# The input projection of a decoder step by a Strassen scheme: seven half-width products in place of eight

## The chip, the cores and the metric

The kernel runs on one core of one Trainium2 chip. The metric is the device time of one execution in microseconds (us). TensorE multiplies, VectorE and ScalarE read its banks in PSUM and work on SBUF, GpSimd clears buffers and issues gathers, and the queue of SP issues most DMA transfers. All numbers of the computation are f32.

## What is computed

One layer for a prompt of 256 tokens and 64 sample tokens (8 requests of 8 tokens), with 2048 features. The part that matters here is the first projection, and what is taken from it:

```python
h = rmsnorm(x, lw['g_attn_norm'])
z = h @ w_in            # 2048 x 4656; columns: q 1024, kc vc ks vs kw vw 256 each, gates 48, u 1024, v 1024
q_rot = partial_rope(q, q_pos)          # also for ks and kw
u = gelu(u)
v = rmsnorm(gelu(v), lw['g_sgu_v'])
```

After it come the compression of cached keys and values, selected and windowed attention, a gated mixing of tokens, an output projection, attention to a memory of 256 tokens (its keys and values are projected ahead of `h @ w_in`) and a mixture of 16 experts.

## The kernel before

The kernel is a row of blocks of code, one for each stage, with a barrier of all engines between them. In the first stage the inputs are normalised and transposed into `hT` (128 lanes x 16 chunks x 320 tokens: feature chunks on the lanes), and the memory's keys and values are made in `mem_kv`. The second stage is the input projection. Its start is at 80.5 us of the profile and the barrier behind it ends at 424 us.

The 4656 columns are worked on in ten blocks, in the order Q0, KS, Q1, KW, KC_, V2, V1, UV, GU, U1. The first five are 512 columns wide, V2 is 416 and the others are 420. A block's weights are 16 chunks of 128 features by its columns. They lie in one of two buffers: `wbuf[0]` is `raw`, which the next stage fills with gathered cache pages, and `wbuf[1]` is `w_in1`. `load(n)` on SP (L426) fetches block n once block n-2 has been multiplied, so it is a block ahead.

For each block `multiply(n)` on TensorE makes three outputs: the prompt's token tiles 0 and 1 (128 tokens each, 16 matmuls of the whole width, L490), and tile 2 with the 64 sample tokens, whose two halves of the columns go to the two halves of the lanes (32 matmuls, L494). Tile r is in bank `4 * (n % 2) + r`. ScalarE takes them from there (L562, with the gelu for u and v), and VectorE takes tile 1 of the blocks KS, KW and KC_ (L610), makes `QR` from `QQ` and applies the rope to q, ks and kw (L592 to L595).

After the blocks KS, KW and KC_ TensorE also turns finished rows into columns, in `turn_blocks(n)` (L506). Each job is up to four transposes into bank 3 or bank 7, by turns, and a copy out of it by `copy_jobs` (L396): even jobs by ScalarE, odd ones by VectorE. A job waits until the job two before it is copied:

```python
if k >= 2:
    pe.wait_ge(copied[k % 2], k // 2)
```

Jobs 0 and 1 are the memory's keys (`m_jobs`, within KS), 2 to 7 are q of Q0 (within KS), 8 to 13 are q of Q1 (within KW), 14 to 16 are the keys (KC_). On VectorE `take(n)` and then `copy_jobs(n)` follow each other for each block. After UV the position rows of the compression are transposed (`pe_terms`, L513), after GU they are multiplied (`pe_sums`, L520), and at the end turned into a column (`pe_columns`, L526). SP stores finished keys and values between its loads, and after the load of V1 it loads the weights of the compression. ScalarE's queue issues two copies of cached windows from DRAM to DRAM (4 MB each) once the first tile is made. GpSimd clears the unused lanes of `QQ` and `Z` at the start (L468, L469) and issues the first two gathers of cache pages into `raw` (L205) when the last block that uses `raw` is multiplied. `vjunk` takes the squares of v, which nothing reads.

Of the kernel before, what the change touches and what calls it, by code (L numbers as in the profile page):

```python
# [21 lines left out]
P = 128  # L22
KC = D // P
# [25 lines left out]
IN_COLS = 4656  # L49
NMEM = 256  # L50
# [99 lines left out]
def trunk(nc, A, out, scratch, const_at):  # L150
    top = ExitStack()
    with top:
# [30 lines left out]
        ident = cst("ident")  # L183
        gain_attn = sb(top, "gain_attn", [P, KC])
# [15 lines left out]
        raw = raw_scope.enter_context(nc.sbuf_tensor("raw", [P, 2, STRIDE * KVW], F32, side="right"))  # L200
        raw_loaded = [sem(f"raw_loaded{u}", True) for u in range(2)]

        def gather_cmp(pool, turn):
# [8 lines left out]
        pe_rows, peT, pe_bias = right("pe_rows", [KC, 2, P]), right("peT", [P, 2, KC]), right("pe_bias", [P, 2])  # L212
# [5 lines left out]
                in_scope.enter_context(nc.sbuf_tensor("w_in1", [P, KC, 512], F32, side="right"))]  # L218
        w_in = w_view("w_in")
        w_in_loaded = sem("w_in_loaded")  # L220

        with ExitStack() as scope:
# [4 lines left out]
            ms = sb(scope, "start_ms", [P, 5])  # L227
# [15 lines left out]
            with nc.Block() as block:  # L243
                @block.sync
                def _(sp):
# [11 lines left out]
                    sp.dma_start(const[:, P:], A["const"][:, P:]).then_inc(const_loaded, 16)  # L257
# [6 lines left out]
                    sp.dma_start(wbuf[0][:, :, :], w_in[:, :, 0:512]).then_inc(w_in_loaded, 16)  # L264
# [92 lines left out]
        with ExitStack() as scope:  # L357
            QQ, QR = (w1[:, :, :, :].rearrange("p u c n -> p (u c n)")[:, a:a + TILES * 512].rearrange("p (r n) -> p r n", n=512) for a in (0, TILES * 512))
            vgain = sb(scope, "vgain", [P, SW])
            ta = sb(scope, "rope_a", [P, 128])  # L360
            tb = sb(scope, "rope_b", [P, 128])
            vjunk = sb(scope, "vjunk", [P, SW])
            vms = sb(scope, "vms", [P, TILES])
            loaded = [w_in_loaded, sem("w_in_loaded1")]
            ready = [sem(f"w_in_ready{u}") for u in range(2)]
            taken_a, taken_d, roped, turned, v_squared, v_scaled, v_rooted, v_ready, gated, vgain_loaded, state_out, blank_q = (sem("w_in_" + x) for x in (
                "taken_a", "taken_d", "roped", "turned", "v_squared", "v_scaled", "v_rooted", "v_ready", "gated", "vgain_loaded", "state_out", "blank_q"))
# [7 lines left out]
            for n, k in ((V2, 4), (V1, 3), (UV, 2), (U1, 1), (GU, 0)):  # L375
                COLS[n] = (Q_COLS + GUV[k], GUV[k + 1] - GUV[k])
# [12 lines left out]
            JOBS = {KS: m_jobs + q_jobs(0), KW: q_jobs(1), KC_: k_jobs}  # L389
            J_BEFORE = {n: sum(len(JOBS.get(m, ())) for m in range(n)) for n in range(NT_IN + 1)}  # L390
# [7 lines left out]
            with nc.Block() as block:  # L398
                @block.sync
                def _(sp):  # L400
# [21 lines left out]
                    def load(n):  # L422
                        a, width = COLS[n]
                        if n >= 2:
                            sp.wait_ge(ready[n % 2], TILES * (n // 2))
                        sp.dma_start(wbuf[n % 2][:, :, 0:width], w_in[:, :, a:a + width]).then_inc(loaded[n % 2], 16)  # L426

                    load(1)
                    sp.dma_start(vgain[:, :], A["g_sgu_v"][0].partition_broadcast(P)).then_inc(vgain_loaded, 16)
                    for n, kind in enumerate(("mem_k_p", "mem_v_p")):  # L430
                        for r in range(2):
                            store(out[kind][0, 0, r * P:(r + 1) * P].rearrange("r h d -> r (h d)"),
                                  mem_kv[:, r, n * MW:(n + 1) * MW])
                    for n in range(2, NT_IN):
                        load(n)
                        done = n - 2
                        if done in (KS, KW, KC_):
                            sp.wait_ge(taken_a, done + 1)
                            sp.wait_ge(taken_d, done + 1)
                            if done != KC_:  # L440
                                sp.wait_ge(roped, done + 1)
# [11 lines left out]
                        if n == V1:  # L453
# [21 lines left out]
                def _(pe):  # L475
                    def multiply(n):
# [3 lines left out]
                        if n >= 2:  # L480
                            pe.wait_ge(taken_a, n - 1)
                            if n - 2 <= KC_:
                                pe.wait_ge(taken_d, n - 1)
# [2031 lines left out]
```

## Time and profile before

| | us |
|---|---|
| median of 3 runs | 1654.53 (1652.16 to 1656.22) |
| the profiled execution | 1652.59 |
| its span, first to last instruction | 1650.8 |
| the input projection with its barrier (80.58 to 424.04) | 343.46 |
| TensorE busy in it | 336.11 |
| VectorE busy in it | 22.79 |
| ScalarE busy in it | 32.50 |

An f32 matmul has two records in the profile, one for each of its passes, and a transpose has one. The records overlap, so the pace of a series is read from the starts of its groups, not from the mean duration. "PEld" is the load of the stationary operand, and "x" counts records. The mean granted clock of TensorE over the whole span is 0.924 of 2.4 GHz.

### The profile page before, as it was taken

The numbers are of one execution on the slowest core, as the hardware profiler recorded it, in microseconds if no ns is written. First come the engines' busy times: TensorE is split into PE (matmuls) and PEld (weight loads), VectorE is DVE, ScalarE is ACT, GpSimd is POOL, SyncE is SP. The second block draws the span as 40 slices with busy tenths as digits, with TensorE's granted clock in tenths as the row PEclk, the third lists the DMA queues.
The fourth block names the chain that finished last, engine by engine and source line by source line (L and its number), as shares of the span: only waits on it lengthen the run. The fifth ranks groups of instructions, "written<-read, shape, count | busy, mean of one in ns | idle before, by whom it ended". The sixth has DMA issues, their size and how long they took to land. (4 is left out here: it accounts for less than half of the span.)

```text
span 1650.8 us, 19858 instructions
## 1 busy us (share of the span) xinstructions
PE 1443.3 (87%) x7384; PEld 794.2 (48%) x7385; DVE 387.3 (23%) x972; ACT 296.7 (18%) x667; POOL 83.5 (5%) x111
## 2 busy tenths in 40 slices
PE   7999999999999988878899999859879978699890
PEld 4444445556788756644444575533323333233330
DVE  3101010000365265466310212521100100101015
ACT  3000000011333234357100113201000000000001
POOL 0000000000200000000000000001001010010100
PEclk9999999999999689979899999969989988899895
DMA  9276224252242077500943222979998999979975
GB/s 357 104 303 254 103 99 139 99 173 103 103 153 65 22 220 229 158 12 1 340 135 110 94 102 103 388 276 401 392 415 307 414 404 388 416 309 414 414 299 195
DMA packets 112657, 371.89 MB, mean 225 GB/s; under 512 B 17331, under 2 KB 55259, under 8 KB 82919
## 3 DMA queue, kind: packets, MB, share of 16 engines
q1 hardware_dynamic: 106898, 334.88, 53.5%
q0 software_dynamic: 5552, 27.89, 4.9%
q10 hardware_dynamic: 144, 8.26, 1.2%
q8 instruction: 42, 0.69, 0.2%
q14 instruction: 21, 0.17, 0.0%
HBM read 394.60 MB, written 26.49 MB: 255 GB/s over the span
## 5 line engine op out<-in xcount | busy, mean ns | idle before, releaser
L2359 PE MATMUL bank<-ring,hT_e 128*64 x576 | 251.7, 595 | 8.2 <-DMA ring<-in_w_exp_up 6.8
L2360 PE MATMUL bank<-ring,hT_e 128*64 128x512 f32 x576 | 251.9, 595 | 0.0
L2376 PE MATMUL bank<-W,const 128*64 128x512 f32 x576 | 150.2, 677 | 53.1 <-DMA W<-in_w_exp_down 48.6
L2359 PEld LDWEIGHTS bank<-ring,hT_e 128*64 128x64 f32 x576 | 78.5, 138 | 167.7 <-issue 167.7
L490 PE MATMUL bank<-raw,hT 128*128 128x512 f32 (+1 forms) x320 | 131.6, 573 | 0.6 <-PEq L243 0.6
L490 PE MATMUL bank<-w_in,hT 128*128 128x512 f32 (+2 forms) x320 | 123.7, 547 | 0.0
L2376 PEld LDWEIGHTS bank<-W,const 128*64 128x64 f32 x576 | 45.0, 155 | 145.0 <-issue 100.5
L1715 PE MATMUL bank<-W,mixT 128*128 128x512 f32 x256 | 113.4, 603 | 1.6 <-DVE mixT L1950 1.6
L490 PEld LDWEIGHTS bank<-raw,hT 128*128 128x128 f32 x320 | 61.5, 193 | 67.5 <-issue 67.3
L490 PEld LDWEIGHTS bank<-w_in,hT 128*128 128x128 f32 x320 | 60.4, 190 | 61.0 <-issue 61.0
L1715 PEld LDWEIGHTS bank<-W,mixT 128*128 128x128 f32 x256 | 49.0, 193 | 63.5 <-issue 61.4
L2360 PEld LDWEIGHTS bank<-ring,hT_e 128*64 128x64 f32 x576 | 78.5, 138 | 0.0
L2422 DVE SCALAR_TENSOR_TENSOR gate<-bank,row_w,gate 64x512 f32<-64x512 f32 x18 | 13.6, 757 | 257.8 <-ACT gate L2402 257.8
L2428 DVE COPY const<-bank 128x512 f32<-128x512 f32 x18 | 12.4, 692 | 198.9 <-PE bank L2376 198.9
L2402 ACT ACTIVATE gate<-bank 64x512 f32<-64x512 f32 x18 | 10.6, 589 | 244.2 <-PE bank L2360 244.2
L2336 POOL DMA_INDIRECT scratch_moe_y<-const,to_row x36 | 35.9, 998 | 365.8 <-DVE const L2428 360.3
L732 PE MATMUL bank<-const,rawg 128*128 128x128 f32 (+1 forms) x320 | 48.0, 273 | 3.2 <-ACT rawg L792 3.2
L2348 PE MATMUL bank<-const,x 64*128 64x64 f32 x304 | 37.9, 277 | 13.2 <-DMA x<-scratch_hn,from_row 13.2
L2348 PEld LDWEIGHTS bank<-const,x 64*128 64x128 f32 x304 | 35.3, 202 | 28.2 <-issue 28.2
L2407 ACT COPY const<-bank 128x512 f32<-128x512 f32 x18 | 10.6, 586 | 198.2 <-PE bank L2376 198.2
L732 PEld LDWEIGHTS bank<-const,rawg 128*128 128x128 f32 (+1 forms) x320 | 39.4, 152 | 12.5 <-ACT rawg L792 3.3
L999 PE MATMUL bank<-const,k_in 128*128 128x128 f32 x192 | 30.1, 306 | 14.3 <-DVE keyT L1079 4.8
(403 smaller groups left out, 1782.5 us busy)
## 6 DMA issues: line engine op xcount, KB each, us to landing
ring<-in_w_exp_gate SPq DMA_DIRECT2D x80, 1024.0 KB
ring<-in_w_exp_up SPq DMA_DIRECT2D x72, 1024.0 KB
W<-in_w_exp_down SPq DMA_DIRECT2D x72, 1024.0 KB
raw<-in_w_in SPq DMA_DIRECT2D x3, 4096.0 KB
W<-in_w_out SPq DMA_DIRECT2D x3, 4096.0 KB, 13.3
w_in<-in_w_in SPq DMA_DIRECT2D x2, 4096.0 KB, 14.7
k_in<-in_cache_sel_k SPq DMA_DIRECT2D x64, 128.0 KB
v_in<-in_cache_sel_v SPq DMA_DIRECT2D x64, 128.0 KB, 3.5
```

The lines of the kernel that those rows point to most:

```text
L490: mm = pe.matmul(bank[4 * u + r][:, 0:width], hT[:, c, r * P:(r + 1) * P], w, start=(c == 0), stop=(c == KC - 1))
L732: mm = pe.transpose(bank[k % LEAD][:, g * n:g * n + n], rawg[0:n, q // 4, a:a + P], ident[0:n, 0:n])
L999: mm = pe.transpose(bank[4 + n % 2][:, k * P:k * P + P], k_in[:, 4 * m + k, c * P:c * P + P], ident)
L1715: mm = pe.matmul(to, hT[:, c, r * P:r * P + P], w(c, slice(0, 512)), start=(c == 0), stop=(c == chunks - 1))
L2336: pool.indirect_dma_start(out=y_rows, out_offset=bass.IndirectOffsetOnAxis(ap=to_row[:, u, h:h + 1], axis=0), in_=y[:, u, h, :], in_offset ...
L2348: mm = pe.transpose(bank[6 + h][:, k * NS:k * NS + NS], rows_in[:, 8 * h + k:D:KC], ident[UP, UP])
L2359: pe.matmul(bank[4 + u][0:NS, :], hT[:, u, c, :], w_g[:, c, :], start=(c == 0), stop=(c == KC - 1))
L2360: mm = pe.matmul(bank[4 + u][UP, :], hT[:, u, c, :], w_u[:, c, :], start=(c == 0), stop=(c == KC - 1))
L2376: mm = pe.matmul(bank[2 * u + n // 2][lane, :], actT[:, q, :], w_d[:, q, 512 * n:512 * n + 512], start=(q == 0), stop=(q == 3))
L2402: act.activation(gate[UP, :], bank[4 + u][0:NS, :], ACT.Silu).then_inc(silu_ready, 1)
L2422: dve.scalar_tensor_tensor(out=gate[UP, :], in0=bank[4 + u][UP, :], scalar=row_w[UP, bass.ds(turn, 1)], in1=gate[UP, :], op0=ALU.mult, op1 ...
L2428: dve.tensor_copy(y[:, u, 1, :], bank[2 * u + 1]).then_inc(y_copied_d, 1)
```

## The change

The prompt's two token tiles and a block of the weights are seen as a 2 x 2 product: tokens 0 and 1, features in two halves of 8 chunks, columns in two halves. In place of the eight products of half width, seven are made, in Winograd's form. `sum_tokens()` makes four sums of the tokens' halves once (S1 to S4, into `s1`, `s4`, the memory's key space `mem_kv` and tile 1 of `hT`), `sum_weights(n)` makes four sums T1 to T4 of the weights' quarters for each block on VectorE, and `add_up(n)` puts the outputs together from the banks and from four products or partial sums that ScalarE copies out of the banks. In the names below C11, C12, C22 and C21 are these outputs.

Around it, the blocks are nine: 512 columns as before for the first five, then four of 524 (V1, UV, GU, U1). The weights have one buffer, `raw_wide`, loaded in two halves of 8 chunks, and the former second buffer holds T1 to T4. The memory's keys are transposed ahead of block 0 and stored first. On VectorE the order in the turn of block n is `sum_weights(n)`, then `take` and `copy_jobs` of block n-1, then `add_up(n)`. `pe_terms` and `pe_sums` move behind the last block. The loads of the compression's weights move to the turn of U1, and the first gathers wait for the last block's P3 and T4. A part of `const` serves as working space in this stage and is loaded from DRAM in the next one. The gelu of u and v is done over `Z` in `finish(n)` for the prompt's tiles.

```diff
+        def load_in(sp, v, a, width):
+            rows = slice(8 * v, 8 * v + 8)
+            sp.dma_start(raw_wide[:, :].rearrange("p (c n) -> p c n", n=IN_WIDE)[:, rows, 0:width],
+                         w_in[:, rows, a:a + width]).then_inc(w_in_loaded[v], 16)
...
-            GUV = [C_G, C_G + 420, C_G + 840, C_G + 1260, C_G + 1680, Z_COLS]
-            Q0, KS, Q1, KW, KC_, V2, V1, UV, GU, U1 = range(10)
+            GUV = [C_G, C_G + IN_WIDE, C_G + 2 * IN_WIDE, C_G + 3 * IN_WIDE, Z_COLS]
+            Q0, KS, Q1, KW, KC_, V1, UV, GU, U1 = range(9)
...
-            JOBS = {KS: m_jobs + q_jobs(0), KW: q_jobs(1), KC_: k_jobs}
+            JOBS = {FIRST: m_jobs, KS: q_jobs(0), KW: q_jobs(1), KC_: k_jobs}
+            THIRD, P1, P2, P5, P6, P3, P7, P4 = range(1, 9)
...
                     def load(n):
...
+                        sp.wait_ge(ready, made(n - 1, P1))
+                        sp.wait_ge(w_summed, added(n - 1, T3))
+                        load_in(sp, 0, *COLS[n])
+                        sp.wait_ge(ready, made(n - 1, P3))
+                        sp.wait_ge(w_summed, added(n - 1, T4))
+                        load_in(sp, 1, *COLS[n])
...
-                        if n == V1:
+                        if n == U1:
+                            sp.wait_ge(v_squared, TILES)
                             for u, kind in enumerate("kv"):
...
-                    pool.wait_ge(ready[0], TILES * (NT_IN // 2))
+                    pool.wait_ge(ready, made(NT_IN - 1, P3))
+                    pool.wait_ge(w_summed, added(NT_IN - 1, T4))
...
+                        def product(to, left, right, start=True):
+                            for c in range(8):
+                                mm = pe.matmul(to, left(c), right(c), start=(start and c == 0), stop=(c == 7), skip_group_check=True)
+                            mm.then_inc(ready, 1)
...
+                        for c in range(KC):
+                            if c % 8 == 0:
+                                pe.wait_ge(w_in_loaded[c // 8], 16 * n + 16)
+                            for h in range(2):
+                                mm = pe.matmul(b[64 * h:64 * h + 64, :], hT[:, c, 2 * P:2 * P + NS], w[:, c, h * half:(h + 1) * half],
+                                               start=(c == 0), stop=(c == KC - 1))
...
+                        product(a, lambda c: hT[:, c, 0:P], lambda c: w[:, c, 0:half])
...
+                        product(c_, lambda c: hT[:, 8 + c, 0:P], lambda c: w[:, 8 + c, 0:half])
+                        pe.wait_ge(x_summed, 4)
+                        pe.wait_ge(kept, copied_out(n, K_THIRD))
+                        pe.wait_ge(w_summed, added(n, T1))
+                        product(b, lambda c: s1[:, c // 4, c % 4, :], lambda c: w_sum[:, 0, c, 0:half])
+                        pe.wait_ge(kept, copied_out(n, K_P1))
+                        pe.wait_ge(w_summed, added(n, T2))
+                        product(a, lambda c: s2[:, c // 4, c % 4, :], lambda c: w_sum[:, 1, c, 0:half], start=False)
+                        pe.wait_ge(kept, copied_out(n, K_P5))
+                        product(b, lambda c: s4[:, c // 4, c % 4, :], lambda c: w[:, 8 + c, half:width], start=False)
+                        pe.wait_ge(kept, copied_out(n, K_U2))
+                        pe.wait_ge(w_summed, added(n, T3))
+                        product(a, lambda c: s3[:, c // 4, c % 4, :], lambda c: w_sum[:, 2, c, 0:half], start=False)
+                        pe.wait_ge(summed, added(n, C11))
+                        pe.wait_ge(w_summed, added(n, T4))
+                        product(c_, lambda c: hT[:, 8 + c, P:2 * P], lambda c: w_sum[:, 3, c, 0:half])
...
+                    turn_blocks(FIRST)
                     for n in range(NT_IN):
                         multiply(n)
                         turn_blocks(n)
-                        if n == UV:
-                            pe_terms()
-                        if n == GU:
-                            pe_sums()
+                    pe_terms()
+                    pe_sums()
                     pe_columns()
...
+                    def sum_weights(n):
...
+                        dve.wait_ge(w_in_loaded[0], 16 * n + 16)
+                        dve.tensor_tensor(t(0), part(0, 1), part(0, 0), ALU.subtract).then_inc(w_summed, 1)
+                        dve.wait_ge(w_in_loaded[1], 16 * n + 16)
+                        dve.wait_ge(w_summed, added(n, T1))
+                        dve.tensor_tensor(t(1), part(1, 1), t(0), ALU.subtract).then_inc(w_summed, 1)
+                        dve.tensor_tensor(t(2), part(1, 1), part(0, 1), ALU.subtract).then_inc(w_summed, 1)
+                        dve.wait_ge(w_summed, added(n, T2))
+                        dve.tensor_tensor(t(3), t(1), part(1, 0), ALU.subtract).then_inc(w_summed, 1)
...
+                    def add_up(n):
...
+                        dve.wait_ge(kept, copied_out(n, K_P1))
+                        dve.wait_ge(ready, made(n, P2))
+                        out_to(0, 0, c_, p1, ALU.add)
+                        dve.wait_ge(kept, copied_out(n, K_U2))
+                        dve.wait_ge(ready, made(n, P3))
+                        out_to(0, 1, b, u2, ALU.add)
+                        dve.wait_ge(kept, copied_out(n, K_U3))
+                        out_to(1, 1, u3, p5, ALU.add)
+                        dve.wait_ge(ready, made(n, P4))
+                        out_to(1, 0, u3, c_, ALU.subtract)
...
                     for n in range(NT_IN):
-                        if n <= KC_:
-                            take(n)
-                        copy_jobs(dve, dve.tensor_copy, 1, n)
+                        sum_weights(n)
+                        if 1 <= n <= KC_ + 1:
+                            take(n - 1)
+                        if n - 1 in JOBS and n - 1 != FIRST:
+                            copy_jobs(dve, dve.tensor_copy, 1, n - 1)
...
+                        add_up(n)
```

Left out of `sum_weights` here are its waits that a sum of block n-1 has been multiplied before it is written over (T1 on P5, T2 on P6, T3 on P7, T4 on P4 of the block before).

## Rows read from the trace of the kernel before

**Rows 1.** The chain of waits that ended last, its first piece.
```profile
1088.94 0.52 issue
```

**Rows 2.** Windows: length, busy time (records) by engine, granted clock, DMA share, GB/s.
```profile
80.58:424.04 343.46, 336.11 (x1418) 179.75 (x1418) 22.79 (x70) 32.50 (x60) 5.66 (x4) 0.99 0.42 153
...
231.80:236.80 5.00, 4.62 (x10) 2.35 (x10) 0.76 (x2) 0.37 (x1) 0.00 (x0) 0.50 1.05 396
...
305.00:307.00 2.00, 2.00 (x7) 1.04 (x6) 0.00 (x0) 0.00 (x0) 0.00 (x0) 1.00 1.06 401
...
400.00:405.00 5.00, 5.00 (x15) 2.66 (x14) 0.00 (x0) 0.00 (x0) 0.00 (x0) 1.00 0.01 3
...
1233.40:1238.00 4.60, 4.58 (x12) 1.48 (x14) 0.00 (x0) 0.00 (x0) 0.00 (x0) 0.50 0.99 420
```

**Rows 3.** Timeline of TensorE, input projection: start, duration, group, and its wait.
```profile
115.27 27.73 PE L490 MATMUL bank<-w_in,hT 128*128 128x512 f32 x64
142.94 7.13 PE L494 MATMUL bank<-w_in,hT 128*64 128x256 f32 x64
150.00 1.09 PE L506 MATMUL bank<-const,mem_kv 128*128 128x128 f32 x8
151.62 0.63 PE L506 MATMUL bank<-const,w 128*128 128x128 f32 x4 [0.53 <-ACT mem_kT L396]
...
157.32 27.73 PE L490 MATMUL bank<-raw,hT 128*128 128x512 f32 x64
...
226.76 1.09 PE L506 MATMUL bank<-const,w 128*128 128x128 f32 x8
...
230.75 1.06 PE L506 MATMUL bank<-const,w 128*128 128x128 f32 x8 [1.80 <-DVE qrT L396]
...
232.81 30.53 PE L490 MATMUL bank<-raw,hT 128*128 128x512 f32 x64
...
329.15 22.83 PE L490 MATMUL bank<-w_in,hT 128*128 128x420 f32 x64
351.91 5.90 PE L494 MATMUL bank<-w_in,hT 128*64 128x210 f32 x64
357.74 0.29 PE L513 MATMUL bank<-const,pe_rows 16*128 16x16 f32 x2
...
386.55 7.15 PE L520 MATMUL bank<-w,peT 128*1 128x128 f32 x64
...
422.22 0.38 PE L526 MATMUL bank<-const,rope_a 1*128 1x1 f32 x2
```

**Rows 4.** Timeline of TensorE in the next stage.
```profile
430.75 0.60 PE L749 MATMUL bank<-d_even,w 128*128 128x256 f32 x2
...
431.62 0.58 PE L751 MATMUL bank<-d_odd,w 128*128 128x248 f32 x2
```

**Rows 5.** Timeline of the weight loads, at the same place.
```profile
430.97 0.41 PEld L750 LDWEIGHTS bank<-x_odd,w_both 128*128 128x128 f32 x2
```

**Rows 6.** Groups of VectorE by line and shape: busy, mean ns, idle before.
```profile
L844 DVE TENSOR_TENSOR d_even<-bank,x_odd 128x256 f32<-128x256 f32 x64 | 27.1, 424 | 50.1 <-ACT x_odd L801 49.8
...
L2456 DVE TENSOR_TENSOR x<-x,ring 128x2048 f32<-128x2048 f32 x2 | 4.6, 2291 | 0.1
```

**Rows 7.** Timelines of GpSimd and VectorE in the input projection.
```profile
81.00 3.12 POOL L469 MEMSET Z<- 64x3632 f32 x1
...
227.73 0.23 DVE L592 TENSOR_TENSOR rope_a<-Z,const 128x64 f32<-128x64 f32 x1 [7.23 <-ACT Z L562]
...
230.00 0.69 DVE L396 COPY qrT<-bank 128x512 f32<-128x512 f32 x1
```

**Rows 8.** DMA issues by line: count, KB each, median us to landing.
```profile
w_in<-in_w_in SPq DMA_DIRECT2D x2, 4096.0 KB, 14.7
...
w_in<-in_w_in SPq DMA_DIRECT2D x2, 3360.0 KB, 11.3
```

**Rows 9.** Timeline of GpSimd: the first gather.
```profile
386.93 1.15 POOL L205 DMA_INDIRECT raw<-in_cache_cmp_k,cmp_rows  x1 [302.80 <-PE bank L494]
```

More of the change, by code:

```diff
@@ L263, in _ @@
                     sp.wait_ge(mem_made, 2)
-                    sp.dma_start(wbuf[0][:, :, :], w_in[:, :, 0:512]).then_inc(w_in_loaded, 16)
+                    for v in range(2):
+                        load_in(sp, v, 0, 512)
                     sp.wait_ge(const_loaded, 16 * 5)
@@ L422, in load @@
                     def load(n):
[L423 to L428, printed above, removed]
-                    sp.dma_start(vgain[:, :], A["g_sgu_v"][0].partition_broadcast(P)).then_inc(vgain_loaded, 16)
[L430 to L434, printed above, removed]
+                        sp.wait_ge(ready, made(n - 1, P1))
[4 more added lines that the diff above has]
+                        load_in(sp, 1, *COLS[n])
+                    for r in range(2):
+                        sp.dma_start(out["mem_k_p"][0, 0, r * P:(r + 1) * P].rearrange("r h d -> r (h d)"), mem_kv[:, r, 0:MW]).then_inc(k_out, 16)
+                    sp.dma_start(vgain[:, :], A["g_sgu_v"][0].partition_broadcast(P)).then_inc(vgain_loaded, 16)
+                    for r in range(2):
+                        store(out["mem_v_p"][0, 0, r * P:(r + 1) * P].rearrange("r h d -> r (h d)"), mem_kv[:, r, MW:2 * MW])
+                    for n in range(1, NT_IN):
                         load(n)
@@ L563, in take @@
-                        ins.then_inc(taken_a, 1)
-                    for n in range(NT_IN):
-                        take(n)
+                        u, width = n % 2, COLS[n][1]
+                        half = width // 2
+                        a, b = (bank[4 * u + k][:, 0:half] for k in range(2))
+                        gelu = n > KC_ and n != GU
+                        act.wait_ge(ready, made(n, THIRD))
+                        if n == Q1:
+                            act.wait_ge(turned, J_BEFORE[KS + 1])
+                            act.wait_ge(roped, KS + 1)
@@ new lines, in take @@
+                        for h in range(2):
+                            to, shaped = half_of(n, 2, h)
+                            of = shaped(b[64 * h:64 * h + 64, :])
+                            ins = act.activation(to, of, ACT.Gelu_apprx_tanh) if gelu else act.copy(to, of)
+                        ins.then_inc(kept, 1)
+                        act.wait_ge(ready, made(n, P1))
+                        if n:
+                            act.wait_ge(summed, added(n - 1, C21))
+                        act.copy(kept_p1[:, 0:half], a).then_inc(kept, 1)
@@ new lines, in take, with finish @@
+                        act.wait_ge(ready, made(n, P5))
+                        act.copy(kept_p5[:, 0:half], b).then_inc(kept, 1)
+                        act.wait_ge(ready, made(n, P6))
+                        act.copy(kept_u2[:, 0:half], a).then_inc(kept, 1)
+                        act.wait_ge(ready, made(n, P7))
+                        act.copy(kept_u3[:, 0:half], a).then_inc(kept, 1)
+                    def finish(n):
+                        act.wait_ge(summed, added(n, C21))
+                        if n == GU:
+                            act.activation(Z[:, :, C_U:GUV[1]], Z[:, :, C_U:GUV[1]], ACT.Gelu_apprx_tanh)
+                            act.activation(Z[:, :, C_G:C_G + 48], Z[:, :, C_G:C_G + 48], ACT.Sigmoid).then_inc(gated, 1)
+                            return
+                        z, width = COLS[n][0] - Q_COLS, COLS[n][1]
+                        act.activation(Z[:, 0:2, z:z + width], Z[:, 0:2, z:z + width], ACT.Gelu_apprx_tanh).then_inc(taken, 1)
@@ L567, in _ @@
                         if n == UV:
-                            act.wait_ge(taken_a, n + 1)
+                            act.wait_ge(taken, 2)
                             for r in range(TILES):
@@ L606, in take @@
                             for r in range(TILES):
                                 rope(QR[:, r, :].rearrange("p (h d) -> p h d", d=HD)[:, :, 0:ROT], r, 2 * NJ)
[L608 to L614 removed]
+                        elif n != KC_:
+                            z = COLS[n][0] - Q_COLS
```

197 lines of the change are left out of this document (112 added, 85 removed).

## The prediction

> **What bounds the kernel now.** I began with the chain of waits. It reaches back only to 1088.94 us [rows 1], so it says nothing of the input projection. A stage that the chain leaves out may still be in series with all that follows, and the windows decide that: from the first multiply of the input projection to the first instruction after its barrier there are 343.46 us, and TensorE is busy for 336.11 of them, at a granted clock of 0.99 [rows 2]. So TensorE is the bound of this stage, every microsecond taken from it comes off the end, and VectorE (22.79 us busy) and ScalarE (32.50 us) have room. The barrier after the stage makes it serial with the rest.
>
> The timeline of TensorE gives the terms. A block of 512 columns takes 27.67 us for the two prompt tiles (115.27 to 142.94) and 7.06 us for the sample tile (142.94 to 150.00). A block of 420 takes 22.76 and 5.83 us [rows 3]. There are five of the first kind, four of the second and one of 416 columns. The stretches between blocks are the breaks in which TensorE turns q or k into columns: 150.00 to 157.32 and 226.76 to 232.81.
>
> **The products.** Before, 32 matmuls a block: 27.67/32 = 0.865 us for 512 columns. After, 56 of half width. The stage after has 256-column f32 matmuls, each with weights of its own: from 430.75 to 431.62 two of them pass, 0.435 us each [rows 4]. Half of 0.865 is 0.432, so half width costs half. The weight load stays hidden there, but narrowly: two loads take 0.41 us beside 0.435 us of streaming [rows 5]. Five blocks cost 5 x 56 x 0.435 = 121.8 us, four of 524 columns 4 x 56 x 0.435 x 262/256 = 99.7, together 221.5. Before it was 5 x 27.67 + 4 x 22.76 + 22.76 x 416/420 = 251.9. **Gain 30.4 us** (31.8 with 0.432; bounds below). The sample tile's columns are the same: 64.4 before, 5 x 7.06 + 4 x 7.06 x 262/256 = 64.2 after, **0.2 us gained**. That one block fewer exists saves nothing else, since blocks without a break follow each other without a gap [rows 3].
>
> **Sums of the tokens and weights, on VectorE.** Each block adds four sums of 2048 elements a lane (2096 in the wide ones): 2.29 us each for two SBUF inputs [rows 6], 9.2 a block. Four more combine the products, 0.42 us each with one input in PSUM [rows 6]. That is 11 us of 31 in a block. The queue order sets what this costs: VectorE finishes the last output of block n-1 (0.1 us after its last product, plus 0.42), then makes T1 to T4 of block n, ready about 3, 5, 7.5 and 10 us into it. TensorE needs T1 only after the sample tile and two products (7.06 + 2 x 3.48 = 14.0 us), T2, T3 and T4 3.5, 10.4 and 13.9 us later. Hidden by 7 us and more; without that cover they would cost up to 9.2 a block. In block 0 VectorE waits for GpSimd's memset, which ends at 84.1 [rows 7], copies 0.7, then makes four token sums of 1024 elements (half of 2.29 and a hand-over, 1.25 each, [rows 6]): T1 stands at about 92.5, wanted at 80.6 + 1.1 + 14.0 = 95.7. It must also wait for the store of the memory keys out of the space of S2; that store is now first in SP's queue, and it has until about 91 before it shows. I take nothing for it. ScalarE's four copies of kept products each have a whole product (3.5 us) before their bank is written again; nothing. Its later gelu pass over Z reads a finished block while the next block's sample tile runs; nothing.
>
> **The loads.** Before, a block's 4 MB were loaded a block ahead into another buffer and landed in 14.7 us, 3360 KB in 11.3 [rows 8], with 20 us to spare. Now the buffer is single and comes in halves. The first half is asked for after product P1, 20 us ahead. The second is asked for after P3, with P7 and P4 (6.96) and half the sample tile (3.53) to come: 10.4 us. At 401 GB/s [rows 2] 3.44 MB need 8.6 us, so 2.7 of the 11.3 are fixed; half a block (2.10 MB) is then 5.2 + 2.7 = 7.9 us. Bounds: 7.35 (half of 14.7) and 14.7. I take 7.9, nearest to the rows at full rate, so 2.5 us of cover and nothing on the path. The page "DMA: Bandwidth & Descriptors" of the Trainium skill, in its part on fixed cost, puts about 2 us on each transfer whatever its size, so cutting a load in two pays it twice; by that figure the half lands after 2 + (14.7 - 2)/2 = 8.4 us, an estimate, and the sum stays as it is, since 8.4 is under 10.4 too.
>
> **The breaks.** Here the change pays. In the breaks after KS and KW, TensorE alternates banks 3 and 7, and transposes k+2 wait until k is copied out; the odd ones are VectorE's. In the new order of VectorE the copies of block KS come in the turn of Q1, behind all four weight sums and the rope of KS. So from the end E of the last product: last output E + 0.5; four sums of 2.29 and their hand-overs, E + 9.8; rope of three tiles as in the KW break, 227.73 to 230.00, 2.27, E + 12.1; from the first copy to the next multiply as there too, 230.00 to 232.81, 2.81 us [rows 3, 7]. The break is 14.9 us. Before, without the memory's transposes, it was 157.32 - 151.62 = 5.7 for KS and 6.05 for KW. **Cost 9.2 + 8.85 = 18.0 us.** Queued behind it are the multiplies of Q1 and of KC_, and so everything. The break after KC_ has three jobs only, none waits for an odd copy, so it stays. The memory's transposes move ahead of block 0 and lose their wait: 1.62 becomes 1.09, **0.5 gained**.
>
> **The clock.** In the KW break TensorE waited 1.80 us in one go and its clock then stood at 0.50 (1.2 GHz) for 5 us; the next block took 30.53 us in place of 27.7, so 2.8 lost [rows 2, 3]. After a wait for a load in the last stage it stood at 0.50 for 4.6 us [rows 2]. The KS break, of the same shape, lost nothing before. Now each contains 11 us of idling, so I charge both: **2.8 us more** for KS, KW keeps its own (bounds 0 and 5.6 for the two). The Trainium skill, page "TensorE: Matmul & The Clock Gate", section "HAM oscillation", says that an engine left idle goes back to half rate and that each burst after a wait starts cold. By it alone the charge would be certain for both breaks, by the rows it is likely (one break of two fell); the sum is the same.
>
> **The tail.** The position terms (two transposes, 64 records from 386.5, two columns) were in TensorE's stream between blocks, 0.22 + 7.1 us. They now stand behind the last product in a chain of engines: last output 0.5, copy 0.2, sums 7.1, two copies 0.5, columns and copy 0.8, against 7.3 + 0.6 + 0.2 before: **1.4 us more**. The gathers for the next stage were issued at 386.93, 35 us before the stage's end, and had landed by 400 [rows 2, 9]. Now they go out after P3 of the last block, 7 us before its end, and with 13 us for both they land about 6 us after it, while the tail and barrier take 10.5. Hidden; without the tail some 3 us would show. SP's extra load of constants in the next stage is waited for only by SP.
>
> **Sum.** -30.4 - 0.2 - 0.5 + 18.0 + 2.8 + 1.4 = **-8.9 us**. The profiled execution took 1652.6 us (span 1650.8), 1.9 under the median of 1654.5; I forecast 1652.6 - 8.9 = **1644 us**. A measurement here tells apart about 0.3%, 5 us.
>
> **Rivals.** *Late second halves (the other side).* Six blocks follow another without a long break (KS, KW, V1, UV, GU, U1). If the half lands x us past 10.4, the stage loses 6x. At 14.7 us, the upper bound, that is 26 us: 1670. It is measurably slower (over 1659.5) from a landing of 13.1 us on (6 x 2.7 = 16). For it: the window copies of ScalarE's queue run beside block KS, and stores of finished blocks follow the loads. Against: 401 GB/s in the rows, and stores come behind.
> *The weight loads show at half width.* 504 matmuls are 1008 records; 10 ns more in each is 10 us. The 0.41 us for two loads [rows 5] leave 12 ns a record before that begins. At 0.225 us a record the time is 1652, at 0.235 it is 1662. In the rows the 256-wide ones come in threes between transposes, never 56 in a row, so it isn't excluded. The Trainium skill, page "TensorE: Matmul & The Clock Gate", section "Back-to-back issue gap", makes the spacing in a stream of load and multiply pairs depend on both, which speaks against halving the width; the rows show it hidden.
> *The gain goes to breaks.* If each break costs 4 us more (a longer chain, a clock that stays low for 10 us in place of 5), the rest is within noise: 1652.
> *The breaks are cheap.* No loss of clock in either and 2 us less in each chain: 1634 to 1638.
>
> **Chances.** Forecast as summed 0.55 (its own range 1638 to 1649); gain eaten by breaks 0.16; late halves 0.11; weight loads 0.10; cheap breaks 0.08. Faster: 0.55 + 0.08 = 0.63. Slower: about half of the two dear rivals, 0.10. Same: the rest, 0.27. The range 1636 to 1657 leaves out part of the cheap case and the far ends of the two dear ones.
>
> **What would show it.** Products at 0.435 us a matmul; a break of 14.9 us after KS and KW with the transposes waiting for a VectorE copy, and a block at 0.50 after each; no wait of TensorE on the load of w_in; 7 us of 128-column records after the last product. The prediction is wrong if a block without a break lasts longer than 24.4 + 7.1 us, or if the wait in a break ends on something else than VectorE's copy.

## The result and the profile after

The change makes the kernel slower. After it the median is 1667.35 us (five runs, 1666.6 to 1673.17), before it 1654.53 us (five runs, 1652.16 to 1658.32). The ratio is 1.0092, with a 95% interval of 1.0073 to 1.0111. Forecast was 1644. "Faster" and "slower" in this document mean that the 95% interval of the ratio leaves out 1; most of the differences are under 2% all the same, this one too.

The profiled execution took 1666.91 us with a span of 1665.1, 14.3 more than before. From the stage's first multiply to the first transposes of the next stage there are 360.78 us (80.28 to 441.06) in place of 345.42 (80.58 to 426.00), 15.4 more. What follows is as long as before (1224.0 and 1224.8 us). So all of the loss is in the input projection.

TensorE's timeline of the kernel after, the rows that answer to [rows 3] (start, duration, group, and in brackets the wait before it):

```profile
80.28 1.06 PE L561 MATMUL bank<-const,mem_kv 128*128 128x128 f32 x8 [0.62 <-PEq L253]
81.28 7.13 PE L527 MATMUL bank<-raw,hT 128*64 128x256 f32 x64
...
136.38 10.04 PE L527 MATMUL bank<-raw,hT 128*64 128x256 f32 x64 [23.61 <-DMA raw<-in_w_in]
146.35 7.17 PE L518 MATMUL bank<-raw,hT 128*128 128x256 f32 x32
...
170.63 1.03 PE L561 MATMUL bank<-const,w 128*128 128x128 f32 x8
...
183.23 1.73 PE L561 MATMUL bank<-const,w 128*128 128x128 f32 x8 [10.66 <-DVE qrT L427]
...
185.74 9.27 PE L527 MATMUL bank<-raw,hT 128*64 128x256 f32 x64
...
250.64 1.03 PE L561 MATMUL bank<-const,w 128*128 128x128 f32 x8
...
265.75 8.52 PE L527 MATMUL bank<-raw,hT 128*64 128x256 f32 x64
...
307.36 7.33 PE L518 MATMUL bank<-raw,hT 128*128 128x262 f32 x32
...
332.32 7.29 PE L527 MATMUL bank<-raw,hT 128*64 128x262 f32 x64
...
428.86 0.29 PE L568 MATMUL bank<-const,pe_rows 16*128 16x16 f32 x2
429.55 7.15 PE L575 MATMUL bank<-w,peT 128*1 128x128 f32 x64 [0.40 <-DVE peT L761]
441.06 2.82 PE L860 MATMUL bank<-const,rawg 128*128 128x128 f32 x12 [3.19 <-ACT rawg L920]
```

Three things are to be seen. A block's seven products take 24.28 us (146.35 to 170.63), or 24.4 where the next sample tile follows at once; a wide one's take 24.96 (307.36 to 332.32). The two breaks, 170.63 to 185.74 and 250.64 to 265.75, last 15.1 us each, and the longest wait in them is for a copy by VectorE. And ahead of block KS TensorE stands still for 23.6 us, waiting for `raw<-in_w_in`. The totals of waits on TensorE between 80 and 441 us (us in all, times, longest) put the same first:

```profile
PE bank L527 <- DMA raw<-in_w_in: 23.6, 1, 23.6
PE bank L561 <- DVE qrT L427: 21.7, 4, 10.7
```

Windows of the kernel after, with the columns of [rows 2]: the whole stage, a piece of the wait, the sample tile behind the wait, and the one behind the KS break.

```profile
80.28:441.06 360.78, 310.64 (x1723) 247.70 (x1723) 122.28 (x144) 41.65 (x81) 7.50 (x5) 0.92 0.41 147
120.00:125.00 5.00, 0.00 (x0) 0.00 (x0) 0.00 (x0) 0.00 (x0) 0.00 (x0) 0.50 0.49 213
136.38:146.35 9.97, 9.97 (x64) 5.76 (x64) 7.06 (x4) 0.00 (x0) 0.00 (x0) 0.70 0.21 79
185.74:194.93 9.19, 9.19 (x65) 5.40 (x64) 0.42 (x1) 0.00 (x0) 0.00 (x0) 0.76 0.01 2
```

TensorE is busy for 310.64 us, some 25 less than before [rows 2]: the multiplications did become fewer. In the piece of the wait no engine works, and yet the DMA engines are busy at a share of 0.49. So the question is what they carry.

The stage's difference, term by term from these rows and those before:

| | us |
|---|---|
| products: 3 x 24.28 + 2 x 24.4 + 4 x 24.96 = 221.5, before 251.9 | -30.4 |
| sample tiles at full clock | -0.2 |
| transposes of the memory's keys, 1.00 for 1.62 | -0.6 |
| two breaks of 15.1, before 5.7 and 6.05 | +18.5 |
| break after KC_, 1.66 for 1.91 | -0.3 |
| clock after the breaks: sample tiles 9.27 and 8.52 for 7.13 (3.5 lost), before 2.8 lost | +0.7 |
| tail, 428.86 to 441.06: 12.2, before 7.3 + 3.78 | +1.1 |
| wait ahead of KS 23.6, and its sample tile 10.04 for 7.13 | +26.5 |
| sum (measured 15.4) | +15.3 |

Without the last row the sum is -11.2; my sum was -8.9. One wait, one time, turned the sign.

### The profile page after: what moved, and what is told of

It is laid out like the page before. It is cut to its first block and busy times, and to the rows that moved or that the text cites. A ratio compares the mean times of both kernels' runs of the same rounds, so it can differ in the third digit from the quotient of the medians.

```text
span 1665.1 us, 20677 instructions
## 1 busy us (share of the span) xinstructions
PE 1413.1 (85%) x7688; PEld 857.7 (52%) x7689; DVE 485.8 (29%) x1045; ACT 303.5 (18%) x687; POOL 83.3 (5%) x111
## 3 DMA queue, kind: packets, MB, share of 16 engines
q10 hardware_dynamic: 144, 8.26, 1.2%
## 5 line engine op out<-in xcount | busy, mean ns | idle before, releaser
L2487 PE MATMUL bank<-ring,hT_e 128*64 x576 | 251.9, 595 | 8.4 <-DMA ring<-in_w_exp_up 7.2
L527 PE MATMUL bank<-raw,hT 128*64 128x256 f32 (+1 forms) x576 | 71.2, 410 | 23.6 <-DMA raw<-in_w_in 23.6
L527 PEld LDWEIGHTS bank<-raw,hT 128*64 128x64 f32 x576 | 43.3, 147 | 49.7 <-DMA raw<-in_w_in 24.0
L518 PE MATMUL bank<-raw,hT 128*128 128x256 f32 (+1 forms) x288 | 65.2, 384 | 0.0
L518 PE MATMUL bank<-w_in,hT 128*128 128x256 f32 (+1 forms) x288 | 64.3, 380 | 0.0
L518 PEld LDWEIGHTS bank<-raw,hT 128*128 128x128 f32 x288 | 54.0, 190 | 11.1 <-issue 3.5
L518 PEld LDWEIGHTS bank<-w_in,hT 128*128 128x128 f32 x288 | 54.5, 189 | 8.4
```

What stands on the lines that cost most here:

```text
L518: mm = pe.matmul(to, left(c), right(c), start=(start and c == 0), stop=(c == 7), skip_group_check=True)
L527: mm = pe.matmul(b[64 * h:64 * h + 64, :], hT[:, c, 2 * P:2 * P + NS], w[:, c, h * half:(h + 1) * half], start=(c == 0), stop=(c == KC - 1))
L2487: pe.matmul(bank[4 + u][0:NS, :], hT[:, u, c, :], w_g[:, c, :], start=(c == 0), stop=(c == KC - 1))
```

## What held the load back

Who issued transfers around it: ScalarE's and SP's queues in the kernel after.

```profile
88.50 1.33 ACTq L598 DMA_DIRECT2D out_win_k_s<-in_cache_win_k  x1
89.86 0.69 ACTq L598 DMA_DIRECT2D out_win_v_s<-in_cache_win_v  x1
```

```profile
96.22 0.39 SPq L229 DMA_DIRECT2D raw<-in_w_in  x1
```

The first half of KS's weights was asked for at 96.22 and multiplied from 136.38, 40 us later; TensorE wanted it at 112.8. The request itself was late. It waits for product P1 and for the sum T3, and in block 0 VectorE's sums start late (it waits for GpSimd's memset first), so that T3 ends at 96.14 only:

```profile
93.85 2.29 DVE L698 TENSOR_TENSOR w_in<-raw 128x2048 f32<-128x2048 f32 x1
```

The two window copies, 8.26 MB from DRAM to DRAM, had been issued 7 us before the request. The view of the DMA queues (packets, MB, share of 16 engines) shows how the two share. q10 has the window copies, q1 the weights. In the kernel after, the windows are 100 to 105, 120 to 125 and 135 to 140 us:

```profile
q10 hardware_dynamic: 16, 1.03, 47.9%
q1 hardware_dynamic: 407, 0.82, 43.3%
...
q10 hardware_dynamic: 16, 1.03, 47.6%
q1 hardware_dynamic: 16, 0.03, 1.7%
...
q1 hardware_dynamic: 500, 1.01, 52.3%
```

At 100 us the two queues together keep 91% of the engines busy: the copies fill half of them (47.9%), and the weights go through the other half (43.3%). At 120 the free half has nothing left to do, so the weights' share on it has landed, and what is left of them stands on the engines of the copies. There each queue moves 16 packets in 5 us, one against one. A packet of the copies has up to 64 KB, one of the weights about 2 KB (1.01 MB / 500). So the weights crawl at 0.03 MB in 5 us until the copies end, at about 130 us. Then they run again, 0.84 MB from 130 to 135 and 1.01 from 135 to 140.

That the DMA engines change queues packet by packet fits the Trainium skill, page "DMA: Bandwidth & Descriptors", section "Queues, rings and completion order", though it puts 9 to 17 descriptors into such a turn; here the recorded packets stand 16 to 16. The same page, section "Why a DMA increments its semaphore by 16 and not by 1", derives the number of engines from the slowest dimension on both sides of the transfer: the largest number up to 16 that divides both. By that rule the copies, whose slowest dimension is 8 requests, get 8 engines, and the trace agrees: from 120 to 125 us both queues together keep 49.3% of the 16 busy, 7.9 engines.

The trace of before shows it too, in the same view. Its load of 115.38 us meets the same copies; the windows are 130 to 135 and 140 to 145 us:

```profile
q10 hardware_dynamic: 16, 1.03, 47.8%
q1 hardware_dynamic: 16, 0.03, 1.7%
...
q1 hardware_dynamic: 479, 0.98, 52.1%
```

Before, this load landed at about 147 us, 32 us after its issue. It was wanted at 157.3, a block ahead and with room, so it cost nothing. The change took that room away.

## The experiments

Times are device medians; where "one run" is said, there is only one. Beside experiments 1 to 4 the kernel before spread from 1640.69 to 1661.7 us in 17 runs, so single runs are read by the length of the stage in their trace (345.4 before, 360.8 after, both from the stage's first multiply to the first transposes of the next stage), which the rest of the kernel doesn't blur. The diffs are shortened and carry comments of mine.

**1. No window copies (one run).** The two copies are left out, so the rows of the windows that they bring to the output are not written.

```diff
-for cache, dst in (("cache_win_k", "win_k_s"), ("cache_win_v", "win_v_s")):
-    act.dma_start(out[dst][0, :, 0:WIN - NT]..., A[cache][0, :, NT:WIN]...).then_inc(window_out, 16)
...
-sp.wait_ge(window_out, 32)
```

> The changed kernel without the two DRAM-to-DRAM copies of cached windows (their rows of the output are left unwritten). Theory A, the copies hold 8 of the 16 DMA engines from 90 to 133 us and the first half of block KS's weights waits behind their long pieces on those engines: the wait of 23.6 us before block KS goes, and with it the 3.0 us that its sample tile lost at half clock; 1667 - 26.6 = 1641 us. Rival B, a half load asked for in the middle of a block is slow by itself or held up by SP's queue: the wait stays and the time is 1667 us.

Measured: 1646.24 us, stage 335.15. The wait is gone, and the sample tile of KS runs at full clock:

```profile
112.50 7.13 PE L527 MATMUL bank<-raw,hT 128*64 128x256 f32 x64
```

**2 and 3. The copies late, in the kernel after and in the kernel before.** SP issues them in the later attention stage, at 696 us in the kernel after and at 707 us in the kernel before; nothing is left out.

```diff
-    act.dma_start(...)          # two window copies, ScalarE, in the input projection
+    sp.dma_start(...)           # the same two, SP, after o_placed in the later stage
```

> The changed kernel with the same two copies issued by SP in the stage at 713 us, where the DMA engines are idle for 70 us. Theory A: as without the copies, 1641 us, no wait before KS. Rival B: 1667 us. A third case, C, that the copies are only moved into another load's way: over 1645 us, with a wait for a load in the later stages that the changed kernel has not.

> The kernel before with the copies issued in the same later place. Theory A: its second load (115 us) is wanted only at 157 us, and the first was in flight ahead of the copies, so it gains nothing: 1654 us, within 3. If the copies cost the kernel before something too (their share of HBM or a slower load), it gets faster by what is charged wrongly to the change.

Measured: the kernel after with late copies 1643.55 us (8 runs), ratio 0.9944 to before (0.9915 to 0.9974), so faster; the kernel before with late copies 1654.2 us (10 runs), ratio 1.0012 (0.999 to 1.0034), no difference. The copies as such cost nothing in either place; in the kernel after they cost about 24 us where they lie, 25.7 in the stage (360.8 to 335.1). The stage of experiment 2 is 10.3 under before. With the breaks and the half clock behind them as they were, this is the kernel that my sum of -8.9 described.

**4 and 5. Smaller pieces (one run each).** What should change is how long one turn of the copies lasts. The pieces are 8 KB, then 2 KB. The edit also changes the slowest dimension, from 8 to 63 and to 252, and with it the number of engines.

```diff
-act.dma_start(out[dst][0, :, 0:WIN - NT].rearrange("b (s t) g d -> b s (t g d)", s=NT), ...)
+act.dma_start(out[dst][0, :, 0:WIN - NT].rearrange("b (s t) g d -> s b (t g d)", t=NT), ...)   # 4: 8 KB
+act.dma_start(out[dst][0, :, 0:WIN - NT].rearrange("b (s t) g d -> s b (t g d)", t=2), ...)    # 5: 2 KB
```

> The changed kernel, copies at their old place, but with the loops of their access exchanged so that a piece is 8 KB and not up to 64 KB. Theory A in its stronger form, an engine takes a piece of each queue by turns, so the length of the other queue's pieces sets the delay: the half load lands in under 20 us and the wait before KS is 0 to 5 us; 1641 to 1648 us. If what counts is only that the engines are shared by bytes, or the copies have precedence: the wait stays above 15 us, 1660 us or more.

> As the run with pieces of 8 KB, but 2 KB. In that run the two queues passed one piece each by turns on the 8 shared engines (118 and 118 in 5 us). Theory A in this form: a piece of 2 KB costs the load only its own time again, so a half block of 64 pieces an engine takes 64 x 2 x 0.15 = 19 us at the most instead of 30, the first half lands at about 114 and the second at about 125; TensorE waits 8 to 12 us in all before and in KS, against 19.6 with 8 KB: 1652 to 1658 us. If the engines are shared by bytes and not by pieces, the wait stays at 19 us and the time at 1667 us.

Measured with 8 KB: 1667.26 us, stage 357.6. The wait did not shrink to 5 us as expected but only from 23.6 to 19.6, and it split in two, one for each half:

```profile
126.27 5.01 PE L527 MATMUL bank<-raw,hT 128*64 128x256 f32 x32 [13.33 <-DMA raw<-in_w_in]
...
137.52 6.20 PE L527 MATMUL bank<-raw,hT 128*64 128x256 f32 x32 [6.24 <-DMA raw<-in_w_in]
```

Its queues from 120 to 125 us say why I was wrong:

```profile
q10 hardware_dynamic: 118, 0.97, 45.6%
q1 hardware_dynamic: 118, 0.23, 11.7%
```

The turns are still one packet against one, 118 to 118, and 8 KB against 2 KB is still four to one. The queues together keep 57.3% of the engines busy, 9.2 of 16, so the copies are on 9 now. That is 118/5/9 = 2.6 packets of weights per engine and us. Half a block is 1024 packets, 64 an engine, so at least 24 us on the shared ones; about 30 passed from the request to the multiply.

With 2 KB, the windows of the copies alone (90 to 95 us), of both queues (115 to 120 us) and of the copies' last stretch (120 to 125 us), and the wait that is left:

```profile
q10 hardware_dynamic: 808, 1.65, 85.2%
...
q10 hardware_dynamic: 433, 0.89, 45.9%
q1 hardware_dynamic: 432, 0.88, 45.6%
...
q10 hardware_dynamic: 762, 1.54, 79.1%
```

```profile
122.09 5.99 PE L527 MATMUL bank<-raw,hT 128*64 128x256 f32 x32 [5.55 <-DMA raw<-in_w_in]
```

The copies now fill 85.2%, some 14 engines, and run at 1.65 MB in 5 us while they are alone; beside the weights the turns are 433 to 432 packets of equal size. A half block then needs 64 packets at 432/5/14 = 6.2 per engine and us, 10.4 us, and the wait has shrunk from 23.6 to 5.55 us, for the second half, which stands behind the first. The expectation had 8 to 12 us of wait, since it took 0.15 us for a piece; by the row it is 0.084 (45.6% of 16 engines for 5 us, over 432 pieces). That kernel took 1654.2 us, stage 342.8, 7.7 over experiment 2. The copies share more engines with the load than in the kernel after and move almost as much beside it (0.89 for 1.03 MB in 5 us), and yet the load is far earlier. Nor did it come earlier because the copies were over: they still moved 1.54 MB from 120 to 125 us, and the load landed at about 122. So the length of the turns makes most of the wait; that the plain sharing of bandwidth makes the rest is inferred, no run isolates it.

The engines of the three versions, 8, 9 and 14, are what the rule of the Trainium skill gives (same page, the section on the semaphore's 16 named above) for slowest dimensions of 8, 63 and 252.

**6. The copies one block later (one run).** If any load of this stage is at risk, the wait should move with the copies. ScalarE issues them once both halves of KS have landed, so they meet the loads of Q1.

```diff
+if n == KS:
+    act.wait_ge(w_in_loaded[1], 16 * n + 16)
+    act.dma_start(...)          # the two window copies
```

> The changed kernel with the window copies issued by ScalarE once both halves of block KS have landed (about 114 us). Theory A: the copies still hold 8 engines for 43 us, until about 158; no wait before KS, but the halves of Q1, asked for at 123 and 137 us, land at about 160, and since VectorE's weight sums of Q1 stand ahead of the copies in the break after KS, that break grows by about 16 us: 1657 us. Rival: a load asked for 20 us ahead and followed by a break of 15 us has cover enough: 1643 us.

Measured: 1663.09 us. The wait ahead of KS is gone, and the break after KS 34.0 us (144.43 to 178.46) in place of 15.1:

```profile
175.94 1.73 PE L561 MATMUL bank<-const,w 128*128 128x128 f32 x8 [29.59 <-DVE qrT L427]
...
178.46 9.88 PE L527 MATMUL bank<-raw,hT 128*64 128x256 f32 x64
```

```profile
161.04 2.29 DVE L692 TENSOR_TENSOR w_in<-raw 128x2048 f32<-128x2048 f32 x1 [16.00 <-DMA raw<-in_w_in]
```

TensorE names VectorE's copy, but that engine itself stands for 16.0 us in `sum_weights` waiting for the load, with the rope and the copies of KS queued behind it. The loss moved with the copies, by 18.9 us where 16 were expected.

**7 and 8. VectorE's order, alone and with late copies.** `sum_weights(n)` goes behind `take` and `copy_jobs` of block n-1.

```diff
-sum_weights(n)
 ...                             # take(n - 1), copy_jobs(n - 1)
+sum_weights(n)
 add_up(n)
```

> The changed kernel with one change of order on VectorE: in the turn of block n it applies the rope and copies the transposes of block n-1 first and makes the four weight sums of block n after that. Theory A, each of the two long breaks (15.1 us) is the four weight sums ahead of the copies: the breaks fall to about 5.7 us, the sums stay hidden, 2 x 9.4 = 18.8 us gained, the wait of 23.6 us before KS stays: about 1648 us. Rival: the sums then come too late for the products of the next block and TensorE waits on VectorE in the block; the gain is under 5 us.

> Both repairs together: the window copies at 713 us and the rope and the copies ahead of the weight sums. Theory A: the gains add, 1643.5 - 18.8 and up to 4 us less lost to the clock after the breaks: 1621 to 1625 us, 1.7 to 2% under the kernel before, and no wait of TensorE over 2 us between 80 and 400 us. Rival: the second half of the next block's weights, which the long breaks covered after KS and KW, now shows there: a wait for w_in of 1 to 3 us after each break.

Measured alone (one run): 1648.55 us. The breaks are 5.58 us (170.17 to 175.75) and 5.94 (240.20 to 246.14), and the wait ahead of KS stays, 23.27. The two losses are thus independent. Together with late copies (4 runs): 1627.86 us, ratio 0.9832 (0.98 to 0.9864), stage 317.35, 17.8 under experiment 2. In the kernel after, VectorE's timeline shows what the order had cost, the four sums between the last product and the first copy of the break:

```profile
170.83 0.42 DVE L711 TENSOR_TENSOR Z<-const,bank 128x256 f32<-128x256 f32 x1 [2.62 <-PE bank L518]
171.17 2.29 DVE L690 TENSOR_TENSOR w_in<-raw 128x2048 f32<-128x2048 f32 x1
...
180.20 0.22 DVE L663 TENSOR_TENSOR const<-Z,const 128x64 f32<-128x64 f32 x1
...
182.48 0.69 DVE L427 COPY qrT<-bank 128x512 f32<-128x512 f32 x1
```

The miss of 3 to 7 us in experiment 8 is partly the clock. Even after the short break the sample tile runs slow, 9.45 us here and 9.83 after KW, 5.0 us lost in the two:

```profile
146.75 1.54 PE L561 MATMUL bank<-const,w 128*128 128x128 f32 x8 [1.82 <-DVE qrT L427]
...
149.07 9.45 PE L527 MATMUL bank<-raw,hT 128*64 128x256 f32 x64
```

**9. Half-width products alone (one run).** The kernel before, with its eight products at half width: the price of a half-width matmul without the scheme.

```diff
-pe.matmul(bank[4*u + r][:, 0:width], hT[:, c, r*P:(r+1)*P], w, start=(c == 0), stop=(c == KC - 1))
+for h in range(2): ...          # c within h
+    pe.matmul(bank[4*u + r][:, h*half:(h+1)*half], hT[:, c, r*P:(r+1)*P], w_half, ...)
```

> The kernel before with each prompt tile of a block made of eight half-width products (64 matmuls of 256 columns or less in place of 32 of the whole width), nothing else changed. Theory A, a matmul of half the width costs half and its weight load stays hidden in an unbroken row of them: a block's prompt tiles take 27.7 to 27.9 us, the kernel 1655 us. So the scheme saves one product in eight. Rival, weight loads show: over 28.5 us a block and over 1660 us.

Measured: 1658.29 us. A block's 64 matmuls take 27.82 us (114.62 to 142.44) where 32 wide ones took 27.67, 0.435 us each:

```profile
114.62 27.89 PE L490 MATMUL bank<-w_in,hT 128*128 128x256 f32 x128
142.44 7.13 PE L500 MATMUL bank<-w_in,hT 128*64 128x256 f32 x64
```

Its stage has 349.3 us, 3.9 more than before: 1.5 by the products of ten blocks, and the rest, some 2.4, by a clock that here fell after the KS break as well (that block has 29.69 us, 157.53 to 187.22).

**10 and 11. Transposes spread out, after and before.** If a break itself costs the clock, it should not be a break. Of the six jobs only two stay between the blocks, two go behind the next sample tile and two behind its first product (in the kernel before: behind tiles of the next block).

```diff
+turn_blocks(n - 1, 1)           # behind the sample tile: two jobs
 ...
+turn_blocks(n - 1, 2)           # behind P1: two jobs
-    for k, (blocks, rows, _) in enumerate(JOBS.get(n, ()), J_BEFORE[n]):
+    if n in (KS, KW):
+        now = len(jobs) - 4
+        jobs = {None: jobs[:now], 1: jobs[now:now + 2], 2: jobs[now + 2:]}[part]
```

> The kernel with both repairs, and of the six transposes jobs after KS and after KW only two are left in the break; two come behind the next block's sample tile and two behind its P1, so that their copies are made while TensorE multiplies. Theory A: each break loses its waits (2.4 us) and with them the fall of the clock (2.4 and 2.8 us lost in the sample tile after it): 1627.9 - 9.5, that is 1616 to 1621 us. Rival: T1 of the next block, which now comes after the last of the spread copies, is late for P5 and TensorE waits there: the same time as without the spreading, 1628 us. Second rival: the clock falls all the same, 1623 us.

> The kernel before with its transposes jobs spread in the same way (the last two pairs behind tiles 0 and 1 of the next block). Theory A: 2 x 2.4 us of waits and the 2.8 us of clock after KW, 7 us gained: 1647 us. If the clock falls at this place whatever the break, 1650 us. It tells how much of the best version is the scheme's and how much the breaks'.

Measured: on top of experiment 8, 1614.07 us (4 runs), ratio 0.9752 (0.9714 to 0.979), stage 305.7; in the kernel before, 1643.89 us (7 runs), ratio 0.9941 (0.9919 to 0.9962). Experiment 10, around what was the KS break:

```profile
144.12 1.03 PE L569 MATMUL bank<-const,w 128*128 128x128 f32 x8
145.09 7.13 PE L527 MATMUL bank<-raw,hT 128*64 128x256 f32 x64
152.15 1.09 PE L569 MATMUL bank<-const,w 128*128 128x128 f32 x8
```

No wait, and 7.13 us, the full clock. The windows from 149 to 154 us set experiment 8 (first) against experiment 10, in the columns of [rows 2]:

```profile
149.00:154.00 5.00, 5.00 (x26) 2.80 (x26) 4.68 (x3) 0.00 (x0) 0.00 (x0) 0.52 0.02 3
```

```profile
149.00:154.00 5.00, 5.00 (x43) 3.62 (x40) 0.69 (x1) 0.58 (x1) 0.00 (x0) 1.00 0.00 0
```

A granted clock of 0.52 in the one is the level of 1.2 GHz, 1.00 in the other that of 2.4 GHz. TensorE had waited 0.24, 1.82 and 0.17 us in the five microseconds before the first, and not at all before the second. Both kernels gained somewhat more than expected: the stages by 11.6 us for 9.5, and by 7.8 (345.4 to 337.6) for 7. Between experiments 10 and 11, which differ by the scheme with its other moves and by the late copies (worth nothing in the kernel before), lie 29.8 us, and 31.9 between their stages. The products' 30.4 are thus there in full; the other moves (the memory's transposes, the tail) about cancel. Experiment 10 is the fastest version, 2.5% under before.

## Why the prediction was wrong

The forecast was faster by 8.9 us; the result was slower by about 13 to 14. The step that failed is **the loads**: "so 2.5 us of cover and nothing on the path".

- **The loads.** I priced a half block at 7.9 us between bounds of 7.35 and 14.7, from landings of transfers that the copies did not hold up: [rows 8] has the landing of the `w_in` line, and none for that of `raw`, where the disturbed load went. For a half alone the price was right: in experiment 2 the packets of the one asked for at 105.22 end between 112 and 113. The half that met the window copies took 40 us. I counted its cover as 20 us; it was 16.5 (96.22 to 112.8), because the request had to wait for T3 as well, but either is far too little. The fixed 2 us that I cited from the Trainium skill are a fit on that page to transfers that GpSimd issues; no run here shows such a part by itself. Experiments 1 and 2 show that the copies are the cause, 4 and 5 that the mechanism is the turns, and 6 that it follows them to another load. As an argument against late loads I used 401 GB/s [rows 2], a mean over 16 engines, 25 GB/s each. The free engines kept nearly that (0.82 MB in 5 us at 43.3% is 24 each), and the half was still not there, because the rest of it stood on the others.
- **The rival, late second halves.** It named the window copies beside KS, but charged second halves of six blocks with one size x up to 14.7. It was one block, and its first half. No other load of the stage made TensorE wait.
- **The products.** Right: -30.4 for -30.4, 24.28 us for seven (0.434 us a matmul). The rival that weight loads show at half width is out: experiment 9 has 0.435 in the kernel before as well.
- **The breaks.** Right: 15.1 us each for 14.9, with TensorE waiting 10.66 for VectorE's copy behind the four weight sums. Experiments 7 and 8 took exactly this back.
- **The clock.** Of the right kind, mis-sized: 3.5 us lost in the two breaks where I summed 5.6 (2.8 kept for KW and 2.8 more for KS), so +0.7 for +2.8. The 11 us of idling, my reason for charging the KS break, are not needed for it: behind waits of at most 1.83 us the clock fell too, in experiments 8 and 9. How much a break loses varies from run to run: in experiment 2, with the same breaks, it was 4.2 us in the two.
- **The tail, the memory's transposes, the sample tile.** +1.1, -0.6 and -0.2 for +1.4, -0.5 and -0.2. The tail's own terms in the prediction add up to 9.1 against 8.1, so to +1.0 and not to +1.4.

With the copies out of the way the forecast was met: experiment 2 has 1643.55 us for 1644, and its stage is 10.3 us shorter for the 8.9 summed. Could it have been seen blind? In kind, yes, and roughly in size. Before, the load issued at 115.38 landed 32 us later, against 10 to 20 us of cover after the change; with all else as summed that gives 1644 + 12 to 22, with 2.9 for the half clock behind the wait 1659 to 1669, an estimate that takes a half block to be held as long as that whole one was: slower, or at the low end on the border of what a measurement tells.

Open stays why the sample tiles behind equal breaks lose between 1.3 and 2.8 us of clock (8.39 us in experiment 5, 9.97 in experiment 1), and why the KS break of the kernel before, with a wait of 1.81 us, lost none while the same break in experiment 9 did.

## What to carry to other kernels

A change that shortens the time between asking for data and using it must be priced with the worst landing in the stage, not with the median: look at the DMA queues in windows, and for each load ask what else is on the engines. A background copy costs nothing as long as every load beside it has tens of us of room; issue it where none is urgent, or in pieces no longer than those of the loads, which here left 5.6 of 23.6 us of wait. And on an engine that works in order, work for the next block goes behind what another engine waits for in this one.

## What was not expected of the hardware

- Two DMA queues on one engine took turns by recorded packets, whatever their size, as the counts of experiments 4 and 5 and of the kernel after show: 16 to 16 in 5 us with up to 64 KB, 118 to 118 with 8 KB, 433 to 432 with 2 KB. A 2 MB load took 40 us beside a copy that used half of the engines.
- The copies from DRAM to DRAM kept to 8 engines (share 0.48) for some 41 us, at 206 GB/s (1.03 MB in 5 us), while the others stood idle once the load's share on them was in. With another order of the same dimensions they were on 14 engines at 330 GB/s (1.65 MB in 5 us).
- TensorE's clock stood at 0.52 after a break with waits of 0.24, 1.82 and 0.17 us, and at 1.00 with the same transposes spread among multiplies. Clock, waits and the gaps of the breaks together were 11.6 us in the stage (317.35 to 305.7), 5.0 of them the clock.
